# Recurrent gate and recurrent output in seven block products each, token-major, with the weight sums on GpSimd, behind the attention branch

## The chip, the cores and the metric

The kernel runs on one core of one Trainium2 chip. The metric is the time of one execution on the device in microseconds, as the median of three runs. One further execution was recorded by the hardware profiler; all rows below come from it.

## The reference, cut to what matters

One decoder layer: 256 tokens and 16 meta tokens ahead of them, width 1024, float32 throughout. A combined input projection feeds latent attention, a gated linear recurrence and two gates; their gated sum goes through an output projection, and a routed expert network follows.

```python
def reference(x, meta_tokens, ...):
    h = concatenate([meta, x], axis=1)                      # 272 tokens
    xn = rms_norm(h, norm_mix_g)
    proj = xn @ w_in                                        # columns: cq, ckv, kr, rx, rg, gates
    attn = mla_branch(proj[cq], proj[ckv], proj[kr], ...)   # ends in  o @ w_ao
    rec = rglru_branch(proj[rx], proj[rg], ...)             # ends in  y @ w_ro
    g = sigmoid(proj[..., OFF_GATE:] + b_gate)
    merged = g[..., :D_MODEL] * attn + g[..., D_MODEL:] * rec
    h = h + merged @ w_out
    h = h + moe_ffn(rms_norm(h, norm_ffn_g), ...)           # top 4 of 32 experts
    return rms_norm(h, norm_final_g)[:, N_META:]
```

Here "recurrent gate" is `sigmoid(xn @ w_in[:, gate columns D to 2D] + b_gate[D:])`, "recurrent output" is `y @ w_ro`, "attention gate" and "attention output" are their counterparts.

## The kernel before, in words

Everything is written out by hand: each engine has one instruction list, and engines wait for one another on counters (`wait_ge`, `then_inc`). The mixer's weights stream through a ring of 16 slots of 1 MB each (`ring`, filled by SyncE in the order of `LOADS`; load n goes out when `weights_used` has reached n - 15). `weights_used` is counted up by TensorE at the first matmul behind the last use of a slot. `M0` is the number of entries of `LOADS`. Behind the mixer the ring and the freed work area hold the experts' weights: 12 pieces (`RING`) of 2.1 MB for two experts at a time. The first twelve are fetched with `fetch` and `fetch_half` as slots and areas come free; the fetches of expert 2 begin when expert 0's pieces are used.

Activations are kept feature-major in the mixer (`xnT`, `gel`, `mT`: features on partitions, tokens along the row). TensorE goes through `jobs` with `project` (L607): a job is 128 output features, eight k-steps, 256 or 272 tokens wide, in PSUM bank n modulo 3. Attention runs in six steps (`attention_step`) hosted by jobs; the linear recurrence (`conv`, `recur_arg`, `recur`) runs on VectorE and ScalarE beside them. ScalarE reads the jobs in order (`read`), so a step's exponentials (`attention_exp`, L1328), which wait for VectorE's row maxima (`rowmax_ready`, L1715), stand ahead of the next job's read (L1288). VectorE walks the same list of jobs.

Then, in TensorE's order: the eight jobs of the recurrent gate (`gr`), the eight recurrent outputs (`recurrent_output`, L829), and two rounds of four attention gate jobs (`ga`) and four attention outputs (L853). ScalarE turns each gate into a tanh; VectorE multiplies it with its branch (`merge_rec`, L1739, and `merge_attn`, L1745 and L1747) and leaves the sum in `mT`.

The output projection is already done in seven products of 128x512 blocks (`product`, L889) in place of eight. `w_out` lies in four blocks of 512x512; VectorE forms five sums of them (L1776 to L1780, 128x2048 each, into `SPARE` or in place) and five sums of the blocks of `mT` (L1785 to L1789), and adds the products into `X` with weights of a half (`add_half`, L1830). Transposes of the new h (`turn_h`, L864), the router and the ranking follow, then the expert loop (L952 to L996).

GpSimd has no work of its own in the kernel.

Of the kernel before, what the change touches and what calls it, by code (L numbers as in the profile page):

```python
# [24 lines left out]
P = 128  # L25
# [111 lines left out]


OUT_BLOCKS = ((1, 1), (1, 0), (0, 0), (0, 1))
# [4 lines left out]
MIX_LANDINGS = [len(range(s, M0, SLOTS)) - (s == 0) for s in range(SLOTS)]  # L144


def load_width(kind, w):
    return {"in": KT * w, "ro": KT * w, "uq": QT * w, "ukv": KVT * w, "ao": 4 * w, "out": 4 * w, "gates": 4 * P}[kind]


def pack_mixer(g):

    packed = np.zeros((M0, P, SLOT), np.float32)
    for n, (kind, a, w) in enumerate(LOADS):
        if kind == "gates":
            both = np.stack([g["w_rg_a"][0, a:a + w], g["w_rg_x"][0, a:a + w]], axis=0)
            flat = both.transpose(2, 0, 1, 3)
        else:
            m = g[{"in": "w_in", "ro": "w_ro", "uq": "w_uq", "ukv": "w_ukv", "ao": "w_ao", "out": "w_out"}[kind]][0]
            if kind == "uq":  # L160
                heads = m.reshape(Q_LORA, 2, HEADS // 2, QD)
                m = np.concatenate([heads[..., :NOPE].reshape(Q_LORA, 2, -1), heads[..., NOPE:].reshape(Q_LORA, 2, -1)], axis=2)
                m = m.reshape(Q_LORA, HEADS * QD)
            m = m.reshape(-1, P, m.shape[1]).transpose(1, 0, 2)
            if kind == "out":
                r, c = OUT_BLOCKS[a]
# [7 lines left out]
def layer(nc, x_in, xT_in, vec_in, ca_in, cb_in, w_mix,  # L174
          norm_ffn_g, w_router, b_router, w_exp, b_up, b_down, norm_final_g, out):
    with ExitStack() as ctx:
# [84 lines left out]
        ta = view(4 * SEQ, LATE + 4736).rearrange("p (k t) -> p k t", k=4)  # L261
# [17 lines left out]
        def out_block(n):  # L279
            s = (M0 - 4 + n) % SLOTS  # L280
            return ring[:, s, :].rearrange("p (k n) -> p k n", k=4)

        w22, w21, w11, w12 = (out_block(n) for n in range(4))
        w12_22 = view(SLOT, SPARE + UNIT).rearrange("p (k n) -> p k n", k=4)
        w21_11 = view(SLOT, SPARE + UNIT + SLOT).rearrange("p (k n) -> p k n", k=4)
# [5 lines left out]
        m21_22 = ca[:, CA["mask"][0]:CA["mask"][0] + 512].rearrange("p (k t) -> p k t", k=4)  # L291
        y2 = hg
# [42 lines left out]
        def col(n):  # L335
# [71 lines left out]
            sem(n) for n in ("wsum_ready", "msum_ready", "product_done"))  # L407
        h_var, h_std, xn2_ready = (
# [32 lines left out]
        jobs += [("gr", i) for i in range(8)] + [("ga", i) for i in range(8)]  # L441
# [5 lines left out]
        hosts = [("rx", 5), ("rx", 7), ("gr", 0), ("gr", 2), ("gr", 4), ("gr", 6)]  # L447
# [4 lines left out]
        def _(spe):  # L452
# [4 lines left out]
            for n, (kind, a, w) in enumerate(LOADS):  # L457
                s = n % SLOTS
                if n == 0:
                    spe.wait_ge(head_in[1], 16)  # L460
                    continue
# [103 lines left out]
        def _(pe):  # L565
# [11 lines left out]
            def wait_load(n):  # L577
                s = slot_of(n)
                pe.wait_ge(slot_loaded[s], 16 * (n // SLOTS + (s > 0)))
# [240 lines left out]
            def recurrent_output(p):  # L820
                n = load_at[("ro", 256 * p)]
                wait_load(n)
                wv = wslot(n, KT)
                if p == 0:
                    pe.wait_ge(recurrence_done, 4)
                for i in range(2):
                    b = branch_begin()
                    for k in range(KT):
                        ins = nc.tensor.matmul(ps[:, b, 0:SEQ], wv[:, k, P * i:P * i + P], gel[:, k, :],  # L829
                                               start=(k == 0), stop=(k == KT - 1))  # L830
                        if k == 0:
                            settle(ins)
                    ins.then_inc(branch_done, 1)
                owed[0] += 1

            for p in range(4):
                for i in (2 * p, 2 * p + 1):
                    project(("gr", i), OFF_GATE + D + P * i, P, N_META, T, last=(i % 2 == 1))
                    if ("gr", i) in step_after:
                        attention_step(step_after[("gr", i)])  # L840
            for p in range(4):
                recurrent_output(p)
            for g in range(2):
                for i in range(4 * g, 4 * g + 4):
                    project(("ga", i), OFF_GATE + P * i, P, N_META, T, last=(i % 2 == 1))
# [3 lines left out]
                pe.wait_ge(attn_ready, NU)  # L849
# [8 lines left out]
                owed[0] += 1  # L858

# [24 lines left out]
            pe.wait_ge(proj_read, len(jobs))  # L884
            pe.wait_ge(wsum_ready, 5)

            def product(bank, m, w, lo=0, hi=4):
                for k in range(lo, hi):
                    ins = nc.tensor.matmul(ps[:, bank, :], m[:, k, :], w[:, k, :], start=(k == 0), stop=(k == 3))  # L889
                    if k == 0:  # L890
                        settle(ins)
                return ins

            pe.wait_ge(branch_read, KT + 4)
            product(4, m11, w12_22).then_inc(product_done, 1)
            pe.wait_ge(branch_read, 2 * KT)
            product(5, m22, w21_11).then_inc(product_done, 1)
            pe.wait_ge(msum_ready, 1)
            product(6, m11_22, w11_22).then_inc(product_done, 1)
            pe.wait_ge(msum_ready, 2)  # L900
            product(0, m11_12, w22).then_inc(weights_used, 1)
            pe.wait_ge(msum_ready, 3)
            product(1, m12, w21, 0, 2)
# [330 lines left out]

        @block.scalar
        def _(act):
# [14 lines left out]
            def read(job):  # L1251
# [44 lines left out]
                elif kind == "gr":  # L1296
# [6 lines left out]
                    ins = nc.scalar.activation(mT[:, i, :], ps[:, b, 0:SEQ], ACT.Tanh, bias=hbg[:, 8 + i:9 + i], scale=0.5)  # L1303
                else:
                    if i >= 4:
                        act.wait_ge(branch_read, 4 + i + 1)
                    ins = nc.scalar.activation(ta[:, i % 4, :], ps[:, b, 0:SEQ], ACT.Tanh, bias=hbg[:, i:i + 1], scale=0.5)
# [23 lines left out]
            def moe_loads(job):  # L1331

                kind, i = job
                if kind == "gr" and i < 4:
                    c, b = i % 2, i // 2
                    act.dma_start(bup[E * i:E * i + E, :], b_up[0, :, F * b + 512 * c:F * b + 512 * c + 512]).then_inc(moe_in, 16)
                if job == ("gr", 4):
                    act.dma_start(wr, w_router[0].rearrange("(k p) e -> p k e", p=P)).then_inc(moe_in, 16)
                if job == ("gr", 5):
                    act.dma_start(brt, b_router[0:1, :].broadcast_to([P, E])).then_inc(moe_in, 16)  # L1340
                if job == ("gr", 6):
                    act.dma_start(upper, cb_in[:, slice(*CB["upper"])]).then_inc(moe_in, 16)
                if job == ("gr", 7):
                    act.dma_start(block_base, cb_in[:, slice(*CB["block_base"])]).then_inc(moe_in, 16)
                if job == ("ga", 0):
                    act.wait_ge(attn_ready, NU)
                    act.dma_start(gffn, norm_ffn_g[0:1, :].broadcast_to([P, D])).then_inc(moe_in, 16)
                if job == ("ga", 1):
                    act.dma_start(slot_id, cb_in[:, slice(*CB["slot_id"])]).then_inc(moe_in, 16)
                if job == ("ga", 2):  # L1350
# [24 lines left out]
            for job in jobs:  # L1375
# [15 lines left out]
                if (job[0] == "rx" and job[1] % 2 == 0 and job[1] > 1) or job == ("gr", 0):  # L1391
                    input_scale(3 if job[0] == "gr" else job[1] // 2 - 1)


# [146 lines left out]
        def _(dve):  # L1541
# [194 lines left out]
            def merge_rec(i):  # L1736
                dve.wait_ge(proj_read, JOB[("gr", i)] + 1)
# [4 lines left out]
            def merge_attn(i):  # L1742
                dve.wait_ge(proj_read, JOB[("ga", i)] + 1)
                dve.wait_ge(branch_done, KT + i + 1)
                link(V.scalar_tensor_tensor(out=ta[:, i % 4, :], in0=ta[:, i % 4, :], scalar=1.0,  # L1745
                                            in1=ps[:, (7, 3)[i % 2], 0:SEQ], op0=ALU.add, op1=ALU.mult))
                V.tensor_tensor(mT[:, i, :], mT[:, i, :], ta[:, i % 4, :], ALU.add).then_inc(branch_read, 1)  # L1747


            gelu_end(0)  # L1750
            for job in jobs[JOB[("ra", 0)]:JOB[("ga", 0)]]:
                kind, i = job
                if job == ("gr", 0):
# [13 lines left out]
                if job == ("gr", 1):  # L1767
                    recur(3)
            for i in range(KT):
                merge_rec(i)  # L1770

            for n in range(4):
                s = (M0 - 4 + n) % SLOTS
                dve.wait_ge(slot_loaded[s], 16 * MIX_LANDINGS[s])
            dve.wait_ge(attn_ready, NU)
            V.tensor_tensor(w12_22, w12, w22, ALU.subtract).then_inc(wsum_ready, 1)  # L1776
            V.tensor_tensor(w21_11, w21, w11, ALU.subtract).then_inc(wsum_ready, 1)
            V.tensor_tensor(w11_22, w11, w22, ALU.add).then_inc(wsum_ready, 1)
# [247 lines left out]
```

## Time and profile before

| | |
|---|---|
| median of three runs | 1159.88 us (1159.43 to 1160.18) |
| profiled execution | 1158.32 us, span 1156.5 us |
| granted clock of TensorE | 0.998 |
| TensorE, VectorE, ScalarE, GpSimd busy | 97%, 21%, 16%, 0% of the span |
| read from memory | 440.5 MB, mean 382 GB/s with the writes |
| first `gr` job on the chain | 116.9 us |
| output products begin | 225.5 us |
| first expert matmul (L977) | 261.2 us |

The span is the time from the first to the last instruction of the profiled execution; its own time has 1.8 us more around it. A matmul of float32 appears in the records as two entries. Busy times are those of the records, and a record's duration can run past the start of the next one; the pieces of the chain do not overlap and are what durations are taken from.

### The profile page before, as it was taken

What the parts mean: (1) busy time and instruction counts of PE and PEld (TensorE: products, weight loads), DVE (VectorE), ACT (ScalarE), POOL (GpSimd) and SP (SyncE); (2) the same over time, 40 slices, a digit from 0 to 9 for tenths busy, and PEclk for the clock granted to TensorE, in tenths of its full rate; (3) what the DMA queues carried; (4) which work ended last, traced back from release to release, by engine and by line L of the source; (5) the groups of instructions that cost most, each with busy time, mean ns of one, the idle gap of its engine ahead of it and who ended that gap; (6) DMA issues with size and microseconds to landing.
All of it is one profiled execution on the core that took longest, in us unless ns stands there. A gap on an engine that the chain in (4) does not pass through costs nothing.

```text
span 1156.5 us, 13260 instructions
## 1 busy us (share of the span) xinstructions
PE 1122.5 (97%) x5576; PEld 519.7 (45%) x5576; DVE 245.2 (21%) x546; ACT 187.8 (16%) x402; POOL 0.2 (0%) x4
## 2 busy tenths in 40 slices
PE   9999999999999999999999999999998989899987
PEld 7778888753433343434333333333333333333422
DVE  5657404351111111111121111111111111111112
ACT  2466600021101010101111110101010101010102
POOL 0000000000000000000000000000000000000000
PEclk9999999999999999999999999999999999999999
DMA  9944425699999999999999999999999999999996
GB/s 346 421 179 159 160 96 224 231 334 349 429 430 430 430 427 439 430 430 433 434 433 431 433 432 432 434 434 433 432 432 432 433 433 434 433 425 430 428 428 281
DMA packets 31317, 442.13 MB, mean 382 GB/s; under 512 B 4720, under 2 KB 5232, under 8 KB 8752
## 3 DMA queue, kind: packets, MB, share of 16 engines
q1 hardware_dynamic: 28224, 438.37, 90.0%
q10 hardware_dynamic: 3056, 3.23, 0.9%
q8 instruction: 28, 0.46, 0.2%
q14 instruction: 9, 0.07, 0.0%
HBM read 440.53 MB, written 1.05 MB: 382 GB/s over the span
## 4 chain that ended last, share of the span: by engine, by line
PE 72%; DMA 25%; ACT 2%; DVE 1%; issue 0%; SPq 0%; another core or an unknown queue 0%; ACTq 0%; DVEq 0%
PE ps L977 28%; DMA work<-in_w_exp_dram 20%; PE ps L996 13%; PE ps L607 9%; DMA ring<-in_w_exp_dram 4%; PE ps L964 4%; PE ps L952 4%; PE ps L829 2%; PE ps L889 2%; PE ps L923 2%; PE ps L853 1%; ACT work L1435 1%; PE ps L692 1%; PE ps L986 1%; PE ps L645 1%; PE ps L958 1%
## 5 line engine op out<-in xcount | busy, mean ns | idle before, releaser
L977 PE MATMUL ps<-ring,work 128*64 128x512 f32 x1536 | 340.9, 595 | 12.6 <-DMA ring<-in_w_exp_dram 12.5
L977 PEld LDWEIGHTS ps<-ring,work 128*64 128x64 f32 x1536 | 108.8, 137 | 229.0 <-issue 216.0
L1921 DVE TENSOR_SCALAR work<-ps 128x512 f32<-128x512 f32 x32 | 22.1, 692 | 724.9 <-PE ps L977 724.9
L607 PE MATMUL ps<-work,ring 128*128 128x256 f32 (+1 forms) x560 | 125.9, 384 | 0.0
L977 PE MATMUL ps<-work 128*64 128x512 f32 x512 | 115.9, 596 | 3.8 <-DMA work<-in_w_exp_dram 3.8
L996 PE MATMUL ps<-ring,work 128*64 128x512 f32 x512 | 113.8, 595 | 4.0 <-ACT work L1435 3.8
L996 PE MATMUL ps<-work 128*64 128x512 f32 x504 | 112.4, 596 | 4.4 <-ACT work L1435 3.8
L607 PEld LDWEIGHTS ps<-work,ring 128*128 128x128 f32 x560 | 105.6, 190 | 17.5 <-issue 1.0
L977 PEld LDWEIGHTS ps<-work 128*64 128x64 f32 x512 | 35.1, 137 | 80.4 <-issue 73.0
L996 PEld LDWEIGHTS ps<-ring,work 128*64 128x64 f32 x512 | 35.2, 137 | 72.0 <-issue 63.0
L964 PE MATMUL ps<-work 64*128 64x512 f32 x256 | 67.5, 627 | 0.0
L996 PEld LDWEIGHTS ps<-work 128*64 128x64 f32 x504 | 34.5, 137 | 71.1 <-issue 61.9
L952 PEld LDWEIGHTS ps<-work 128*128 128x128 f32 x512 | 58.5, 192 | 14.6 <-issue 14.6
L952 PE MATMUL ps<-work 128*128 128x128 f32 x512 | 61.9, 279 | 0.0
L1430 ACT ACTIVATE work<-ps 128x256 f32<-128x256 f32 x33 | 12.7, 384 | 201.9 <-PE ps L958 196.8
L1454 ACT ACTIVATE work<-work 128x512 f32<-128x512 f32 x15 | 9.4, 630 | 206.8 <-DVE work L1921 206.8
L964 PEld LDWEIGHTS ps<-work 64*128 64x128 f32 x256 | 20.8, 185 | 45.9 <-issue 45.9
L923 PE MATMUL ps<-work 32*64 32x512 f32 x256 | 34.8, 613 | 0.0
L829 PE MATMUL ps<-work,ring 128*128 128x256 f32 x128 | 27.9, 378 | 0.0
L1435 ACT ACTIVATE work<-ps 128x256 f32<-128x256 f32 x64 | 21.1, 381 | 30.7 <-PE ps L986 28.1
L1426 ACT ACTIVATE work<-ps 128x512 f32<-128x512 f32 x32 | 19.1, 598 | 42.6 <-PE ps L952 42.6
L1459 ACT ACTIVATE work<-ps 128x512 f32<-128x512 f32 x15 | 9.0, 597 | 103.7 <-PE ps L996 103.7
(273 smaller groups left out, 636.9 us busy)
## 6 DMA issues: line engine op xcount, KB each, us to landing
ring<-in_w_exp_dram SPq DMA_DIRECT2D x40, 4096.0 KB, 42.2
work<-in_w_exp_dram SPq DMA_DIRECT2D x20, 4096.0 KB, 42.1
ring<-in_w_exp_dram SPq DMA_DIRECT2D x38, 2048.0 KB, 18.3
work<-in_w_exp_dram SPq DMA_DIRECT2D x17, 2048.0 KB, 18.8
ring<-in_w_mix_dram SPq DMA_DIRECT2D x28, 1024.0 KB, 9.0
ring<-in_w_exp_dram SPq DMA_DIRECT2D x20, 1024.0 KB, 8.3
work<-in_w_exp_dram SPq DMA_DIRECT2D x13, 1024.0 KB, 10.8
ring<-in_w_mix_dram SPq DMA_DIRECT2D x8, 256.0 KB, 13.4
```

What stands on the lines that cost most here:

```text
L607: ins = nc.tensor.matmul(ps[part:part + width, b, 0:hi - lo], wv[:, k, o:o + width], rows[:, k, lo:hi], start=(k == 0), stop=(k == KT - 1))
L829: ins = nc.tensor.matmul(ps[:, b, 0:SEQ], wv[:, k, P * i:P * i + P], gel[:, k, :], start=(k == 0), stop=(k == KT - 1))
L889: ins = nc.tensor.matmul(ps[:, bank, :], m[:, k, :], w[:, k, :], start=(k == 0), stop=(k == 3))
L923: nc.tensor.matmul(ps[CAP * c:CAP * c + CAP, b, :], sel[E * q:E * q + E, par, :], bup[E * q:E * q + E, :], start=True, stop=False)
L952: ins = nc.tensor.matmul(ps[:, bank, P * j:P * j + P], xn2[:, i, P * (4 * h + j):P * (4 * h + j) + P], pick[:, i, :, :], start=(i == 0), s ...
L964: ins = nc.tensor.matmul(ps[:, 4 + 2 * i + c, :], turned[CAP * c:CAP * c + CAP, i, :], rows[CAP * c:CAP * c + CAP, :], start=False, stop=True,
L977: ins = nc.tensor.matmul(ps[CAP * c:CAP * c + CAP, b, :], xeT[:, k, CAP * (u % 2):CAP * (u % 2) + CAP], wu[:, k % SPAN, 512 * q:512 * q + ...
L996: ins = nc.tensor.matmul(ps[CAP * c:CAP * c + CAP, bank, :], turned[:, j, CAP * g:CAP * g + CAP], wv[:, k, 512 * c:512 * c + 512], start=( ...
L1426: nc.scalar.activation(xeT[:, 4 * h:4 * h + 4, :], ps[:, bank, :].rearrange("p (j t) -> p j t", j=4), ACT.Copy).then_inc(xeT_ready, 1)
L1430: return nc.scalar.activation(turned, ps[:, bank, 0:SEQ].rearrange("p (i t) -> p i t", i=TT), ACT.Copy)
L1435: nc.scalar.activation(turned[:, 2 * h:2 * h + 2, :], ps[:, banks[h], o[h]:o[h] + 256].rearrange("p (j t) -> p j t", j=2), ACT.Copy) .then ...
L1921: V.tensor_scalar(hg, ps[:, 0, :], LIMIT, None, ALU.min).then_inc(glu_ready, 1)
```

## The change

The attention gate takes the place of the recurrent gate in the list of jobs (its eight jobs host the attention steps), both attention output rounds follow, and then the recurrent side comes in a new form, token-major: tokens on partitions, 512 features along the row.

- `w_in`'s recurrent gate columns (`gr`) and `w_ro` (`ro`) are loaded as four blocks of 512x512 each. Two entries `sum` in `LOADS` for each of them reserve a ring slot without a load, so `LOADS` grows from 36 entries to 40.
- Each of the two matrix products becomes seven `token_product`s of four k-steps, 128 tokens by 512 features. Three weight sums (`three`) and a fourth (`fourth`, after the second product) are formed by GpSimd, as are the five sums of `w_out` that VectorE formed before: 13 GpSimd operations of 128x2048.
- VectorE forms the sums of the activation blocks (`row_sums`), reads each product from PSUM and combines them (`gate_sums`, `rec_sums`), with the bias as a row that is broadcast by a new DMA on ScalarE's queue; ScalarE takes the tanh of four quarters; `gated` multiplies gate and branch.
- TensorE turns the four gated quarters back to feature-major (`turn_rec`, four transposes each) and VectorE adds them to `mT` (`add_rec`). The last quarter is turned between the second and the third output product.
- SyncE's fetches of the first two experts wait for other events; the fetch of `gffn` moves behind the second output product.

```diff
-    loads += [("in", OFF_GATE + D + 256 * p, 256) for p in range(4)]
-    loads += [("ro", 256 * p, 256) for p in range(4)]
-    for h in range(2):
-        loads += [("in", OFF_GATE + 512 * h, 256), ("in", OFF_GATE + 512 * h + 256, 256), ("ao", 512 * h, 512)]
+    loads += [("in", OFF_GATE + 256 * p, 256) for p in range(4)]
+    loads += [("ao", 512 * h, 512) for h in range(2)]
+    for g, kind in enumerate(("gr", "ro")):
+        loads += [(kind, 0, 512), ("sum", 2 * g, 0), (kind, 1, 512), (kind, 2, 512), ("sum", 2 * g + 1, 0), (kind, 3, 512)]
...
             for c in range(6):
-                if c == 5:
-                    spe.wait_ge(proj_done, len(jobs))
-                    fetch(1, 0)
                 spe.wait_ge(weights_used, M0 - SLOTS + SPAN * (c + 1))
                 fetch(0, c)
-                if c == 2:
-                    spe.wait_ge(branch_done, KT)
-                    fetch_half(1, 5, 1)
+            fetch_half(1, 5, 1)
+            spe.wait_ge(recT_done, 4)
+            fetch(1, 0)
+            fetch_half(1, 1, 0)
             spe.wait_ge(product_done, 1)
-            fetch_half(1, 1, 0)
-            spe.wait_ge(product_done, 2)
             fetch_half(1, 1, 1)
...
+            def token_product(q, m, w, frees=1):
+                if q >= 4:
+                    pe.wait_ge(token_read, q - 3)
+                product(TOKEN_BANKS[q % 4], m, w).then_inc(token_done, 1)
+                owed[0] += frees
...
+            token_product(0, x11, weight_block("gr", 0))
+            token_product(1, x12, weight_block("gr", 3), frees=0)
+            pe.wait_ge(asum_ready, 1)
+            pe.wait_ge(wsum_ready, 3)
+            token_product(2, asum[:, 1], weight_block("sum", 1), frees=0)
+            token_product(3, x21, weight_block("sum", 0))
+            token_product(4, asum[:, 0], weight_block("gr", 1))
+            token_product(5, asum[:, 2], weight_block("gr", 2))
+            pe.wait_ge(wsum_ready, 7)
+            token_product(6, x22, weight_block("gr", 3), frees=2)
...
+            token_product(7, g11, weight_block("ro", 0))
+            token_product(8, g12, weight_block("ro", 3), frees=0)
+            pe.wait_ge(asum_ready, 2)
+            token_product(9, asum[:, 1], weight_block("sum", 3), frees=0)
+            token_product(10, g21, weight_block("sum", 2))
+            pe.wait_ge(branch_read, KT)
+            turn_rec(0)
+            token_product(11, asum[:, 0], weight_block("ro", 1))
+            token_product(12, asum[:, 2], weight_block("ro", 2))
+            turn_rec(1)
+            pe.wait_ge(wsum_ready, 13)
+            token_product(13, g22, weight_block("ro", 3), frees=2)
+            turn_rec(2)
...
+        @block.gpsimd
...
+            def three(kind, g):
+                loaded(kind)
+                pool.wait_ge(weights_used, LOAD_AT[("sum", 2 * g + 1)] - SLOTS + 1)
...
+                combine(third, b22, b12, ALU.subtract)
+                combine(b12, b12, b11, ALU.subtract)
+                pool.wait_ge(wsum_ready, done[0])
+                combine(second, b22, b12, ALU.subtract)
...
+            def fourth(kind, g):
+                pool.wait_ge(token_done, 7 * g + 2)
+                b21 = weight_block(kind, 3)
+                combine(b21, weight_block("sum", 2 * g + 1), b21, ALU.subtract)
...
+            three("gr", 0)
+            three("ro", 1)
+            fourth("gr", 0)
+            loaded("out")
+            pool.wait_ge(attn_ready, NU)
+            pool.wait_ge(branch_done, KT)
+            pool.wait_ge(recurrence_done, 4)
+            combine(w12_22, w12, w22, ALU.subtract)
+            combine(w21_11, w21, w11, ALU.subtract)
+            combine(w11_22, w11, w22, ALU.add)
+            combine(w21, w21, w22, ALU.add)
+            combine(w12, w11, w12, ALU.add)
+            fourth("ro", 1)
...
+            for j in range(4):
+                act.wait_ge(gate_summed, j + 1)
+                nc.scalar.activation(quad(j), quad(j), ACT.Tanh, scale=0.5).then_inc(gate_tanh, 1)
+            act.wait_ge(product_done, 2)
+            act.dma_start(gffn, norm_ffn_g[0:1, :].broadcast_to([P, D])).then_inc(gffn_in, 16)
...
+            def row_sums(a11, a12, a21, a22):
+
+                link(V.tensor_tensor(asum[:, 0], a21, a22, ALU.add))
+                link(V.tensor_tensor(asum[:, 1], asum[:, 0], a11, ALU.subtract))
+                link(V.tensor_tensor(asum[:, 2], a12, asum[:, 1], ALU.subtract))
+                V.tensor_tensor(a21, a11, a21, ALU.subtract).then_inc(asum_ready, 1)
...
+                link(V.tensor_tensor(t1, token(2), t0, ALU.add))
...
+                link(V.tensor_tensor(t2, t1, b_step, ALU.add))
+                link(V.tensor_tensor(t0, token(3), t1, ALU.add))
+                dve.sem_inc(token_read, 1)
+                link(V.tensor_tensor(t1, t0, b_step, ALU.add))
+                V.tensor_tensor(quad(1), token(4), t1, ALU.add).then_inc(gate_summed, 1)
...
+            row_sums(x11, x12, x21, x22)
+            dve.wait_ge(bias_in, 16)
+            link(V.tensor_tensor(b_step, b_step, b_lo, ALU.subtract))
+            gate_sums()
+            row_sums(g11, g12, g21, g22)
+            rec_sums()
+            dve.wait_ge(recT_read, 2)
             V.tensor_tensor(m11_22, m11, m22, ALU.add).then_inc(msum_ready, 1)
```

`link` makes VectorE wait for its own operation before the next one.

## Rows read from the trace of the kernel before

**Rows 1.** The page: busy time by engine, transfer rate in 40 slices.
```profile
PE 1122.5 (97%) x5576; PEld 519.7 (45%) x5576; DVE 245.2 (21%) x546; ACT 187.8 (16%) x402; POOL 0.2 (0%) x4
...
GB/s 346 421 179 159 160 96 224 231 334 349 429 430 430 430 427 439 430 430 433 434 433 431 433 432 432 434 434 433 432 432 432 433 433 434 433 425 430 428 428 281
```

**Rows 2.** Windows: stretch, length, busy by engine, granted clock, DMA share, GB/s.
```profile
225.00:240.00 15.00, 15.00 (x38) 6.82 (x37) 8.88 (x18) 0.00 (x0) 0.00 (x0) 1.00 0.83 311
...
285.00:300.00 15.00, 15.00 (x74) 5.01 (x72) 0.00 (x0) 0.60 (x1) 0.00 (x0) 1.00 1.03 430
...
909.00:938.00 29.00, 26.76 (x144) 11.54 (x142) 3.78 (x8) 3.08 (x6) 0.00 (x0) 1.00 1.01 434
```

**Rows 3.** The chain that ended last: start us, us, what.
```profile
116.92 3.45 PE ps L607 x16
...
156.34 27.73 PE ps L829 x128
...
225.50 15.45 PE ps L889 x36
...
261.15 3.58 PE ps L977 x16
```

**Rows 4.** The same chain, pieces from 88 to 128 us.
```profile
94.02 0.18 DVE small L1715
...
96.72 1.73 PE ps L791 x6
...
114.98 1.94 PE ps L791 x8
...
123.20 0.81 PE ps L776 x6
```

**Rows 5.** Timeline of TensorE in the output products: start us, us, what.
```profile
240.79 0.60 PE L864 MATMUL ps<-ca,work 128*128 128x128 f32 x4
241.23 1.88 PE L889 MATMUL ps<-ring,work 128*128 128x512 f32 x4
```

**Rows 6.** Timeline of VectorE, one weight sum and two sums of `mT`.
```profile
184.51 2.29 DVE L1776 TENSOR_TENSOR work<-ring 128x2048 f32<-128x2048 f32 x1
...
226.53 0.69 DVE L1785 TENSOR_TENSOR work<-work 128x512 f32<-128x512 f32 x1
227.14 0.69 DVE L1786 TENSOR_TENSOR work<-work 128x512 f32<-128x512 f32 x1
```

**Rows 7.** Timeline of SyncE's queue, and issue to landing of L465 from 95 to 125 us.
```profile
98.94 0.80 SPq L465 DMA_DIRECT2D ring<-in_w_mix_dram  x2
...
DMA to landing us min/median/max: 4.7/4.7/7.2
...
138.91 0.33 SPq L465 DMA_DIRECT2D ring<-in_w_mix_dram  x1
...
156.80 28.06 SPq L473 DMA_DIRECT2D ring<-in_w_exp_dram  x3
```

**Rows 8.** Timeline of VectorE from 103 to 116 us.
```profile
103.73 1.58 DVE L1619 SCALAR_TENSOR_TENSOR work<-work,vec 128x272 f32<-128x272 f32 x3
...
109.92 1.08 DVE L1706 SCALAR_TENSOR_TENSOR work<-ps,ca 128x288 f32<-128x288 f32 x2
...
112.15 0.17 DVE L1715 TENSOR_SCALAR small<-small 128x4 f32<-128x4 f32 x1
...
115.73 0.35 DVE L1726 TENSOR_SCALAR work<-work,small 128x256 f32<-128x256 f32 x1
```

**Rows 9.** Timeline of ScalarE: exponentials, then the next read.
```profile
112.36 0.42 ACT L1328 ACTIVATE work<-work,small 128x144 f32<-128x144 f32 x1 [1.88 <-DVE small L1715]
...
114.18 0.36 ACT L1288 ACTIVATE work<-ps 128x256 f32<-128x256 f32 x1
```

**Rows 10.** An issue on ScalarE's queue (KB, us to landing); VectorE's first use of `gffn`.
```profile
ca<-in_ca_dram ACTq DMA_DIRECT2D x1, 505.0 KB, 8.9
...
248.97 1.29 DVE L1824 SCALAR_TENSOR_TENSOR work<-work,small 128x1024 f32<-128x1024 f32 x1
```

More of the change, by code:

```diff
@@ L276, in layer, with weight_block @@
         counts = view(E, 0)
[L279 to L285, printed above, removed]
+        def weight_block(kind, a):
+            return ring[:, LOAD_AT[(kind, a)] % SLOTS, :].rearrange("p (k n) -> p k n", k=4)
+        w22, w21, w11, w12 = (weight_block("out", n) for n in range(4))
+        w12_22 = view(SLOT, SPARE + UNIT + SLOT).rearrange("p (k n) -> p k n", k=4)
+        w21_11 = view(SLOT, SPARE + 2 * UNIT).rearrange("p (k n) -> p k n", k=4)
         w11_22 = view(SLOT, SPARE + 3 * UNIT).rearrange("p (k n) -> p k n", k=4)
@@ L440, in layer @@
                 jobs += [(kind, i) for kind in kinds for i in (2 * p, 2 * p + 1)]
-        jobs += [("gr", i) for i in range(8)] + [("ga", i) for i in range(8)]
+        jobs += [("ga", i) for i in range(8)]
         JOB = {job: n for n, job in enumerate(jobs)}
@@ L818, in branch_begin, with product @@
                 return (7, 3)[d % 2]
[L820 to L842, printed above, removed]
+            def product(bank, m, w, lo=0, hi=4):
+                for k in range(lo, hi):
+                    ins = nc.tensor.matmul(ps[:, bank, :], m[:, k, :], w[:, k, :], start=(k == 0), stop=(k == 3))
+                    if k == 0:
+                        settle(ins)
+                return ins
+            for i in range(KT):
+                project(("ga", i), OFF_GATE + P * i, P, N_META, T, last=(i % 2 == 1))
+                if ("ga", i) in step_after:
+                    attention_step(step_after[("ga", i)])
             for g in range(2):
-                for i in range(4 * g, 4 * g + 4):
-                    project(("ga", i), OFF_GATE + P * i, P, N_META, T, last=(i % 2 == 1))
                 n = load_at[("ao", 512 * g)]
@@ L881, in fold @@
                 nc.tensor.matmul(ps[:, (1, 3)[i], 0:E], logT, pick_e[:, 0:E], start=True, stop=True).then_inc(logits_done, 1)
[L884 to L894, printed above, removed]
+            pe.wait_ge(token_read, 12)
+            pe.wait_ge(recT_read, 1)
             product(4, m11, w12_22).then_inc(product_done, 1)
-            pe.wait_ge(branch_read, 2 * KT)
+            pe.wait_ge(recT_read, 2)
             product(5, m22, w21_11).then_inc(product_done, 1)
+            turn_rec(3)
             pe.wait_ge(msum_ready, 1)
@@ L1232, in _, with combine, loaded @@
                         scatter(1, y, gpickT).then_inc(more_done, 1)
+        @block.gpsimd
+        def _(pool):
+            done = [0]
+            def combine(out, a, b, op):
+                done[0] += 1
+                nc.gpsimd.tensor_tensor(out, a, b, op).then_inc(wsum_ready, 1)
+            def loaded(kind):
+                for a in range(4):
+                    n = LOAD_AT[(kind, a)]
+                    pool.wait_ge(slot_loaded[n % SLOTS], 16 * landings(n))
+            def three(kind, g):
+                loaded(kind)
+                pool.wait_ge(weights_used, LOAD_AT[("sum", 2 * g + 1)] - SLOTS + 1)
+                b11, b12, b22 = (weight_block(kind, a) for a in range(3))
+                third, second = weight_block("sum", 2 * g), weight_block("sum", 2 * g + 1)
+                combine(third, b22, b12, ALU.subtract)
[19 more added lines that the diff above has]
+            fourth("ro", 1)
         @block.scalar
@@ L1750, in _ @@
             gelu_end(0)
-            for job in jobs[JOB[("ra", 0)]:JOB[("ga", 0)]]:
+            for job in jobs[JOB[("ra", 0)]:]:
                 kind, i = job
-                if job == ("gr", 0):
+                if job == ("ga", 0):
                     gelu_end(3)
```

179 lines of the change are left out of this document (128 added, 51 removed).

## The prediction

> **What bounds the kernel now.** I read the page first, for the slices. TensorE is busy 97% of the span and the transfer rate climbs to about 430 GB/s from the ninth slice and stays there [rows 1]. Two stretches follow from it. Up to about 260 us (mixer, router) the transfer engines have room, 311 GB/s at 225 to 240 us, while TensorE is busy in all 15 us; from 285 us they are full, and late in the run TensorE is busy only 26.8 of 29 us beside a DMA share of 1.01 [rows 2]. So the expert stage is bound by transfers: its first matmul is at 261.2 us [rows 3], 30 of the 32 experts' weights (6 pieces of 2.1 MB each, 377.5 MB together) can only be fetched from about then, since the two experts ahead fill the buffers, and 377.5 MB at 432 GB/s are 874 us, which with 261 comes to 1135 us, the tail behind it. What moves the start of the expert stage by x us moves the end by x us, both ways. The chain of waits then says what sets that start: from 98 us on it is TensorE without a gap in the projections and products [rows 3], but just ahead it goes through VectorE and ScalarE: the maxima of the attention rows end at 94.2 us, ScalarE's exponentials and copies follow, and TensorE resumes at 96.7 [rows 4].
>
> **What is removed and added on TensorE.** A projection job of eight k-steps takes 3.45 us and the eight recurrent outputs 27.73 us [rows 3]. Eight gate jobs and the outputs: 27.6 + 27.7 = 55.3 us go. A projection's eight matmuls show as 16 records, two each, so the first 36 records of the output products in 15.45 us are 18 matmuls: 0.86 us each, 3.44 us a product of four [rows 3]. Fourteen products are 48.2 us. Four `turn_rec` of four transposes each: the next product starts 0.44 us behind such a group [rows 5], so 1.8 us. 55.3 - 48.2 - 1.8 = 5.3 us saved. The attention branch keeps its work and only moves; product 0 would begin at 225.5 - 55.3 = 170.2 us, t0 from here on.
>
> **VectorE's new work at its bare price.** A 128x512 operation starts 0.60 us after the one before [rows 6]. 15 of them come with the gate and 20 with the recurrent output, 21 us over 49 us; taken off are five sums of 2.3 us each [rows 6] and 16 short merges. Followed step by step against 3.44 us a product, each bank is read before it is needed again; `row_sums` on `gel` comes after token 6 (t0+24.1), so it begins at t0+24.8, ends at 27.3, and product 9 wants it at t0+31.0: 3.7 us of cover. The additions behind the last product end by +9.7 us, and the halves of h catch up about 1 us before TensorE wants the first for its transpose. Cost nothing, if VectorE runs freely.
>
> **GpSimd.** It has four instructions in the whole trace [rows 1], so no row prices its sums. From below: VectorE's 2.29 us for the same 128x2048 operation [rows 6]. From above I take double, 4.6 us, an estimate for an engine that would take its two inputs one after the other. I use the double; a sum as quick as VectorE's own, on an engine that the kernel leaves idle, seems the less likely end. In a free run the seven sums from the gate's fourth to the output's fourth lie between t0+6.9 (two products done) and t0+45.6 (product 13): covered up to 5.5 us each, so nothing is paid at either end. The Trainium skill, "GPSIMD Engine Reference", § Performance versus the Vector engine, gives 4497 ns for GpSimd and 2293 ns for VectorE at this size; the row agrees with the second, no row shows the first, and by it the sums below would be some 3% smaller.
>
> **The two engines together.** No row shows GpSimd and VectorE working at once. Bounds: they don't touch each other (0), or an operation of one with two SBUF inputs waits until the other's instruction ends. I take the second, worked out at 4.6 us an instruction, because the new GpSimd work lies exactly over VectorE's densest stretch. Two places:
>
> Place A, the gate's first three sums. The load in slot position 29 is issued at 98.9 us and lands 4.7 us later [rows 7], and `weights_used` has reached 14 by then, so `three("gr", 0)` runs from 103.6. VectorE is without a gap from 103.7 to 112.3, and up to 109.9 nearly all its work has two SBUF inputs: convolution steps, scans, products; then come L1706 (one input in PSUM) and L1713 [rows 8]. ScalarE waits in order for the row maxima (released by VectorE at 112.36) and reads the next projection only at 114.18 [rows 9]; TensorE's second `ra` job needs that read at about 115.4 and the chain has it at work from 114.98 [rows 4]. Slack 0.5 us. If each of the three instructions blocks VectorE for its full length: 3 x 4.6 - 0.5 = 13.3 us. If VectorE runs on and GpSimd gets its turn only when L1706 comes, half of the first instruction and what VectorE waits for anyway is covered; the step's probabilities, done at 116.1 us [rows 8] and wanted by the transposes at 123.2 [rows 4], have 7 us of room, and the next step's 5: 4.4 us are left by my count. No row decides the order of turns: I take 9 us.
>
> Place B, `row_sums` on `gel`. Fourth sum of the gate t0+6.9 to 11.5, then VectorE's `t2` add, sum, `t1` add, and so on in alternation: the output sums end at 16.7, 21.9, 26.5. `row_sums` from 24.8: its four linked operations each stand behind one GpSimd instruction, 27.1, 32.3, 37.5, 42.7. Product 9 waits from 31.0 to 42.7: 11.7 us. If GpSimd goes through without yielding, `t2` itself is late and product 7 waits 11 us; same price. Behind VectorE nothing else is queued that TensorE wants sooner. The early three sums of `ro` run at 144 to 158, where VectorE has next to nothing.
>
> Sum: -5.3 + 9 + 11.7 = +15.4 us on the profiled execution's 1158.3 us (span 1156.5 and 1.8 around it) = 1173.7; the median of the runs is 1.6 above that: **1175 us**.
>
> The Trainium skill, "SBUF — State Buffer", § Who interferes with whom, speaks against this change: a VectorE instruction with two SBUF inputs and a GpSimd instruction that reads SBUF exclude each other, the later one waiting for the whole of the earlier. No run here shows it; by that rule the time would be the 1175 us above, and by the profile's silence 1154.6.
>
> **Queues.** The sums take four ring positions, so SyncE's first expert fetch waits for product 3 (t0+14, 184.6 us) and no longer for 156.8, the time of its first one now [rows 7]. All six pieces of expert 0 are out by 220 us; the first half-piece of expert 1 and those after it go at 220 to 251 us, 10.5 MB of 1 MB to 2 MB each, 25 us at 430 GB/s. The last lands at about 255, when expert 0 begins (255.9). Cost 0, about 2 us of cover; each MB late would be 2.4 us. `gffn` moves to ScalarE behind product 5 (7.3 us after the output products begin); a 505 KB transfer on that queue took 8.9 us [rows 10], so it is there at +16.2, and L1824 wants it at +23.5 (248.97 less 225.5) [rows 10]. Cost 0, 7 us of cover. Behind its wait on ScalarE stands nothing due before +18.
>
> **The rivals.** (1) The engines don't disturb each other: -5.3, **1154.6 us**. For it: GpSimd is absent from the trace, so nothing contradicts it. It decides as soon as both stalls together stay under 5.3 us. (2) They take turns but the sums are short (2.29 us) or share in part: A costs 3 x 2.3 - 0.5 = 6.4 at most, B nothing (the last output sum ends at t0+22, before `row_sums`): +1.1, **1161 us**, with 1157 to 1166 around it. (3) GpSimd over 5.5 us a sum, without disturbing VectorE: product 13 waits 7 x (D - 5.5); at 6.2 us the gain is used up and the time is 1159.9. Against it: that is 2.7 times VectorE's row. (4) The saving is real but the late fetches take it: 2.2 MB of backlog, again 1159.9; against it the idle transfer time at 225 to 240 us [rows 2].
>
> **How the numbers follow.** Turns at full price: 0.52, with its own range 1166 to 1180 (A at 4.4 or 13.3). Rival 2: 0.13. Rival 1: 0.30. Rivals 3 and 4: 0.05. 0.2% is 2.3 us, about what a measurement of this kernel can tell. Faster (below 1157.6): rival 1 and a little of 2, 0.31. Same: the middle of rival 2 with 3 and 4, 0.13. Slower: 0.56. The range has to hold both rival 1 and the full price: 1154 to 1180.
>
> **What would show it.** The products' start to the first L977 matmul (35.7 us now) should stay; the stretch from the last `ga` job to the output products should be 5.3 us shorter than its counterpart, plus B. If the engines take turns, VectorE has gaps of about one GpSimd instruction ahead of two-input operations at 104 to 118 us and in `row_sums`, released by nothing that the profile names, and TensorE idles at about 115 and ahead of product 9. If GpSimd's instructions start apart by far less than 4.6 us, or VectorE shows none of these gaps, the forecast is wrong, and the time is near 1155. A long idle of TensorE might also lower its granted clock, which is 1.00 in all stretches named here [rows 2]; I give that nothing.

## The result, and the profile after

The changed kernel takes 1181.3 us (median of four runs, 1179.3 to 1182.3) against 1159.9 us before: ratio 1.0183, 95% interval 1.0165 to 1.0200, or 21.4 us slower. The forecast was 1175 us with a range to 1180; the direction was right, the size was not, and the time lies 1.3 us outside the range. The profiled execution took 1182.2 us, 23.9 us over that of before.

The page after, sections 1 and 2 (answers to [rows 1]): GpSimd now has 61 us of work, and TensorE shows two holes, in slices 5 and 8, each with a lowered granted clock in the same slice.

```profile
PE 1126.2 (95%) x5448; PEld 498.4 (42%) x5448; DVE 278.5 (24%) x560; ACT 186.8 (16%) x398; POOL 61.2 (5%) x17
...
PE   9999699699999999999999999999999999999987
...
PEclk9999799799999999999999999999999999999999
```

Waits of the changed kernel from 100 to 260 us (who waited for whom: us in total, times, longest). TensorE waits for long at two places only.

```profile
ACT work L1427 <- DVE small L1818: 14.5, 1, 14.5
...
PE ps L822 <- ACT work L1392: 12.0, 1, 12.0
...
PE ps L853 <- DVE work L1850: 10.2, 1, 10.2
```

The first is place A of the prediction: TensorE's second `ra` job waits for ScalarE's read, which stands behind the exponentials, which wait 14.5 us for VectorE's row maxima (1.88 us in [rows 9]). The second is place B: product 9 waits for `row_sums` on `gel` (L1850 is its fourth operation). TensorE's timeline at both:

```profile
116.06 0.62 PE L822 MATMUL ps<-work,ring 128*128 128x272 f32 x2
128.69 3.09 PE L822 MATMUL ps<-work,ring 128*128 128x272 f32 x6 [12.01 <-ACT work L1392]
131.57 4.61 PE L638 MATMUL ps<-work,ring 128*128 128x256 f32 x16
...
185.80 31.06 PE L853 MATMUL ps<-ring,work 128*128 128x512 f32 x72
227.07 9.84 PE L853 MATMUL ps<-ring,work 128*128 128x512 f32 x16 [10.21 <-DVE work L1850]
...
237.18 7.03 PE L853 MATMUL ps<-ring,work 128*128 128x512 f32 x16
```

Behind both holes the same work is slower: 16 records of products take 9.84 us at 227 and 7.03 us at 237, so 2.8 us more; at 128.7 the six records of `ra` and `ri` (the recurrence's own small gate matrices, L822) take 3.09 us (1.73 us at 97.97 us in the same trace) and the projection job 4.4 from its start to that of the next work at 136.01 (3.45 in [rows 3]), 2.3 us together. The windows of the changed kernel (columns as in [rows 2]) show the granted clock at 0.54 to 0.60 there, near the lower of the two levels, 1.2 GHz, and back at 1.00 from 234 us. That this is the cause was tested; see the last experiment.

```profile
129.00:134.00 5.00, 5.00 (x13) 3.89 (x13) 2.66 (x8) 3.72 (x9) 0.00 (x0) 0.54 0.11 16
218.00:227.00 9.00, 0.00 (x0) 0.00 (x0) 8.97 (x3) 0.00 (x0) 8.47 (x2) 0.55 0.07 31
227.00:234.00 7.00, 6.93 (x10) 3.02 (x11) 2.49 (x5) 0.00 (x0) 0.00 (x0) 0.60 0.00 0
234.00:249.00 15.00, 15.00 (x45) 7.25 (x44) 6.25 (x10) 0.00 (x0) 0.00 (x0) 1.00 0.53 194
```

GpSimd's timeline: ten of its thirteen sums, in the two places.

```profile
105.19 14.01 POOL L1301 TENSOR_TENSOR ring<-ring 128x2048 f32<-128x2048 f32 x3 [104.74 <-DMA ring<-in_w_mix_dram]
...
192.91 4.52 POOL L1301 TENSOR_TENSOR ring<-ring 128x2048 f32<-128x2048 f32 x1 [17.79 <-PE ps L853]
197.39 14.36 POOL L1301 TENSOR_TENSOR work<-ring 128x2048 f32<-128x2048 f32 x3
211.71 14.76 POOL L1301 TENSOR_TENSOR ring<-ring 128x2048 f32<-128x2048 f32 x3
```

And VectorE's timeline beside them, first place A, then place B. At 105 us the three convolution steps that took 1.58 us in [rows 8] take 9.87, and the product behind them 5.02; at 119.8, when GpSimd is done, the next two-input operation takes 0.72 again.

```profile
104.97 9.87 DVE L1722 SCALAR_TENSOR_TENSOR work<-work,vec 128x272 f32<-128x272 f32 x3
114.76 5.02 DVE L1795 TENSOR_TENSOR work<-work 128x544 f32<-128x544 f32 x1
119.82 0.72 DVE L1796 TENSOR_TENSOR_SCAN work<-work 128x272 f32<-128x272 f32 x1
...
199.81 0.69 DVE L1866 TENSOR_TENSOR work<-ps,work 128x512 f32<-128x512 f32 x1 [1.83 <-PE ps L853]
200.65 2.25 DVE L1868 TENSOR_TENSOR work<-work 128x512 f32<-128x512 f32 x1 [0.15 <-DVE work L1866]
...
210.87 1.43 DVE L1847 TENSOR_TENSOR work<-work 128x512 f32<-128x512 f32 x1 [0.15 <-DVE work L1874]
212.33 4.88 DVE L1848 TENSOR_TENSOR work<-work 128x512 f32<-128x512 f32 x1
217.25 4.87 DVE L1849 TENSOR_TENSOR work<-work 128x512 f32<-128x512 f32 x1
222.15 4.87 DVE L1850 TENSOR_TENSOR work<-work 128x512 f32<-128x512 f32 x1
```

Three things are to be seen. An operation `work<-work` (two inputs in SBUF) beside GpSimd lasts until about the end of the GpSimd instruction that it meets, up to 4.88 us for 0.69 us of work. An operation of the same shape with one input in PSUM (`work<-ps,work`) keeps its 0.69 us while GpSimd is busy. And the waiting stands in the *duration* of the operation, not in the idle time ahead of it: VectorE looks busy (14.9 of 15 us from 105 to 120), and no releaser is named. I had looked for gaps; there are none.

The first expert matmul (L1036) starts at 284.8 us on the chain, 23.6 us later than in [rows 3]: 12.0 and 10.2 of idle, 2.3 and 2.8 of slow clock, less 5.3 saved, make 22.0 (the 5.3 is the prediction's figure; the kernel without GpSimd, below, gives 5.5). Some 1.3 us more had arisen by 98 us, in work that both kernels share; in the eight profiles below TensorE's resumption there ([rows 4]: 96.7) lies between 97.2 and 98.1 us, in the kernel before with small additions too (97.6 and 98.1), so I take it for the scatter of single executions. 0.3 us stay unexplained.

### The profile page after: what moved, and what is told of

Read it like the earlier page. It is cut to its first block, busy times and chain, and to the rows that moved or that the text cites. A ratio compares the mean times of both kernels' runs of the same rounds, so it can differ in the third digit from the quotient of the medians.

```text
span 1180.4 us, 13044 instructions
## 1 busy us (share of the span) xinstructions
PE 1126.2 (95%) x5448; PEld 498.4 (42%) x5448; DVE 278.5 (24%) x560; ACT 186.8 (16%) x398; POOL 61.2 (5%) x17
## 4 chain that ended last, share of the span: by engine, by line
PE 80%; DMA 12%; DVE 4%; ACT 2%; issue 1%; another core or an unknown queue 0%; SPq 0%; ACTq 0%; DVEq 0%
PE ps L1036 33%; PE ps L1055 16%; DMA work<-in_w_exp_dram 11%; PE ps L638 6%; PE ps L853 6%; PE ps L1023 5%; PE ps L1011 5%; PE ps L982 2%; PE ps L869 1%; ACT work L1538 1%; PE ps L1045 1%; PE ps L1017 1%; DVE work L1722 1%; PE ps L723 1%; DMA ring<-in_w_mix_dram 1%
## 5 line engine op out<-in xcount | busy, mean ns | idle before, releaser
L1036 PE MATMUL ps<-ring,work 128*64 128x512 f32 x1536 | 344.3, 599 | 11.9 <-DMA ring<-in_w_exp_dram 11.9
L1036 PEld LDWEIGHTS ps<-ring,work 128*64 128x64 f32 x1536 | 109.8, 138 | 230.6 <-issue 219.2
L1036 PE MATMUL ps<-work 128*64 128x512 f32 x512 | 115.8, 595 | 1.9 <-DMA work<-in_w_exp_dram 1.9
L638 PE MATMUL ps<-work,ring 128*128 128x256 f32 (+1 forms) x432 | 98.9, 388 | 0.0
L638 PEld LDWEIGHTS ps<-work,ring 128*128 128x128 f32 x432 | 82.2, 192 | 14.6 <-issue 1.0
L853 PE MATMUL ps<-ring,work 128*128 128x512 f32 x136 | 62.5, 615 | 10.2 <-DVE work L1850 10.2
L1036 PEld LDWEIGHTS ps<-work 128*64 128x64 f32 x512 | 35.3, 137 | 77.8 <-issue 73.6
L1301 POOL TENSOR_TENSOR ring<-ring 128x2048 f32<-128x2048 f32 x10 | 46.7, 4688 | 165.0 <-DMA ring<-in_w_mix_dram 147.1
L853 PEld LDWEIGHTS ps<-ring,work 128*128 128x128 f32 x136 | 26.5, 198 | 42.4 <-issue 31.3
```

What stands on the lines that cost most here:

```text
L638: ins = nc.tensor.matmul(ps[part:part + width, b, 0:hi - lo], wv[:, k, o:o + width], rows[:, k, lo:hi], start=(k == 0), stop=(k == KT - 1))
L1036: ins = nc.tensor.matmul(ps[CAP * c:CAP * c + CAP, b, :], xeT[:, k, CAP * (u % 2):CAP * (u % 2) + CAP], wu[:, k % SPAN, 512 * q:512 * q + ...
L1301: nc.gpsimd.tensor_tensor(out, a, b, op).then_inc(wsum_ready, 1)
```

## The experiments

Eight kernels, on three chips, each beside the kernel before on the same chip. That took 1159.24 us beside the first four, 1159.64 beside the next three (quarters, GpSimd reading, GpSimd writing) and 1159.96 beside the last.

**Place A alone undone.** GpSimd's first three sums wait until VectorE has finished its last attention step.

```diff
+            pool.wait_ge(probs_ready, NU)
             three("gr", 0)
```

> The changed kernel with one wait more: GpSimd begins the gate's first three sums only when VectorE has finished its last attention step. Theory (the engines take turns, whole instruction by whole instruction, for operations with two SBUF inputs, and TensorE's granted clock falls while it idles): the 12.0 us idle of TensorE at 117 to 129 us and the 2.5 us that the slow clock cost behind it go, the 10.2 us ahead of product 9 and its 2.8 us stay; 1181.3 - 14.5 = 1167 us. Rival (the delay comes from the new order of branches and the new loads, GpSimd only happens to be active then): the stall stays, 1179 to 1182 us. Rival (GpSimd in this place costs only in part): between 1170 and 1178 us.

Measured: 1166.5 us, ratio 1.0066 (1.0051 to 1.0082). The stall at 117 us is gone, the one ahead of product 9 is unchanged at 10.23 us. All six early sums now run from 140.7 to 167.9 us. The reordering as such costs nothing here.

**Place B alone undone.** The two fourth sums and the five of `w_out` go to VectorE, into its waits between the products; `late_sums` counts them in order.

```diff
                 V.tensor_tensor(quad(0), token(1), t0, ALU.add).then_inc(gate_summed, 1)
+                late(weight_block("gr", 3), weight_block("sum", 1), weight_block("gr", 3), ALU.subtract)
...
                 link(V.tensor_tensor(t2, t1, b_step, ALU.add))
+                late(w12_22, w12, w22, ALU.subtract)
...
                 link(V.tensor_tensor(t1, t0, b_step, ALU.add))
+                late(w21_11, w21, w11, ALU.subtract)
...
+                late(w11_22, w11, w22, ALU.add)
                 V.tensor_tensor(quad(2), token(5), t2, ALU.add).then_inc(gate_summed, 1)
+                late(w21, w21, w22, ALU.add)
...
             row_sums(g11, g12, g21, g22)
+            late(w12, w11, w12, ALU.add)
...
                 gated(0)
+                late(weight_block("ro", 3), weight_block("sum", 3), weight_block("ro", 3), ALU.subtract)
```

> The changed kernel with the two fourth sums and the five sums of w_out on VectorE, put into its waits between the products; GpSimd keeps the six early sums. Theory of turns: row_sums on gel is free again and product 9 starts on time; 10.2 us idle and 2.8 us of slow clock go, place A stays: 1181.3 - 13.0 = 1168 us. Rival (VectorE has too much work behind the reordering, GpSimd or not): with seven sums of 2.3 us more on VectorE the products wait longer, 1181 to 1190 us.

Measured: 1167.6 us, ratio 1.0074 (1.0059 to 1.0089). Product 9 starts without a wait, the idle at place A is 11.99 us as in the changed kernel. VectorE has room for 16 us of sums more between the products: the rival of too much work falls.

**Both undone.**

> Both edits of the two runs beside it: early sums on GpSimd while VectorE rests, the late seven on VectorE. Theory of turns: both stalls and both stretches of slow clock go and only the 5.3 us saved on TensorE are left: 1181.3 - 27.5 = 1153.8, against 1159.9 - 5.3 = 1154.6 us by the forecast's own sum; so 1154 to 1155.5 us. Rival (later fetches of the experts take the saving): 1158 to 1161 us. Rival (the two stalls hide a third wait): above 1161 us.

Measured: 1153.4 us, ratio 0.9948 (0.9934 to 0.9961). The two costs add up. Counted from the kernel before on the same chip, the changed kernel is 21.4 us slower, the one without place A 7.3, the one without place B 8.3, and the one without both is 5.9 us faster: 14.1 and 13.1 us, 27.2 together, against 27.3 measured. So no third cost of that size is hidden, and the saving arrives.

**No sum on GpSimd.** The early six go to VectorE too, between its last attention step and the merges.

```diff
+            three("gr", 0)
+            three("ro", 1)
             for i in range(KT):
                 merge_attn(i)
...
-        @block.gpsimd
```

> No sum on GpSimd: the six early sums too are VectorE's, behind its last attention step, where it rests for some 18 us. Theory of turns: the same as with the early sums on a GpSimd that disturbs nobody, 1154 to 1155.5 us. Rival (VectorE is the bound once it has all the sums, 30 us more in 60): 1160 us or more, with waits of TensorE for wsum_ready.

Measured: 1152.9 us, ratio 0.9945 (0.9932 to 0.9959), 6.3 us faster than before and level with the kernel that has both places undone. GpSimd's help was never needed. Rows of the chain of this kernel, to compare with [rows 3]:

```profile
171.24 37.77 PE ps L854 x88
...
256.71 3.58 PE ps L1038 x16
```

From TensorE's resumption at 97.8 us in this trace to the first expert matmul are 158.9 us; before they were 164.4 [rows 3, 4]. 5.5 us, where the sum of the prediction has 5.3.

**The sums in quarters.** The changed kernel, each sum as four instructions of 128x512, the counts that TensorE waits for times four.

```diff
-                done[0] += 1
-                nc.gpsimd.tensor_tensor(out, a, b, op).then_inc(wsum_ready, 1)
+                for k in range(4):
+                    done[0] += 1
+                    nc.gpsimd.tensor_tensor(out[:, k, :], a[:, k, :], b[:, k, :], op).then_inc(wsum_ready, 1)
```

> The changed kernel with every GpSimd sum cut into four instructions of 128x512; same elements, same places. Theory of turns by instruction: a VectorE operation waits for one short GpSimd instruction (4.7/4 = 1.2 us), so the four of row_sums end at about t0+24.8+4x1.8=32 instead of 43 and product 9 is late by 1 us in place of 10; at place A VectorE has ten two-input operations in a row, each behind a 1.2 us instruction, so 10 to 12 us are lost as before. 1181.3 - 9 - 2.8 = 1169.5 us. Rival (shared bandwidth, in proportion to what is moved): both stalls unchanged, 1181 us.

Measured: 1165.5 us, ratio 1.0051 (1.0034 to 1.0068), 4 us below what I expected. At place B the four operations take 0.73 and three times 1.64 us, and product 9 doesn't wait at all (1 us expected). At place A TensorE still idles 8.78 us (10 to 12 expected). Same elements moved, 16 us less lost: what counts is the length of the instruction that VectorE meets, not the traffic. VectorE's timeline in this kernel:

```profile
104.29 3.35 DVE L1723 SCALAR_TENSOR_TENSOR work<-work,vec 128x272 f32<-128x272 f32 x3
107.56 1.79 DVE L1796 TENSOR_TENSOR work<-work 128x544 f32<-128x544 f32 x1
...
114.24 1.36 DVE L1720 TENSOR_SCALAR work<-work,vec 128x272 f32<-128x272 f32 x1
...
207.47 0.73 DVE L1848 TENSOR_TENSOR work<-work 128x512 f32<-128x512 f32 x1 [0.15 <-DVE work L1875]
208.24 1.64 DVE L1849 TENSOR_TENSOR work<-work 128x512 f32<-128x512 f32 x1
...
211.58 1.64 DVE L1851 TENSOR_TENSOR work<-work 128x512 f32<-128x512 f32 x1
```

In a stretch where VectorE has no pause, as at place A, the short turns add up to some three quarters of the long ones; over four operations they don't. The TENSOR_SCALAR at 114.24 has one input tensor in SBUF, with scalars per partition, and takes 1.36 us where it takes 0.42 alone (103.84 us in the same trace): two inputs are not the only form that waits.

**GpSimd reading and writing, in the kernel before.** Six subtractions on GpSimd, which read two inputs and write a result that nobody uses into a borrowed area, begun when the load in position 29 has landed. ScalarE waits for them before it first writes into that area itself; that instruction starts only at 202.9 us, released by TensorE, 82 us behind GpSimd's last (120.6), so the wait costs nothing.

```diff
+        @block.gpsimd
+        def _(pool):
+            scratch = ta.rearrange("p k t -> p (k t)")
+            pool.wait_ge(x_in_s, 16 * TT)
+            pool.wait_ge(slot_loaded[29 % SLOTS], 16 * 2)
+            for n in range(6):
+                if n:
+                    pool.wait_ge(pool_done, n)
+                nc.gpsimd.tensor_tensor(scratch, X[:, 0, :], X[:, 1, :], ALU.subtract).then_inc(pool_done, 1)
...
+                    if i == 0:
+                        act.wait_ge(pool_done, 6)
```

> The kernel before, and on GpSimd six subtractions of 128x1024 from SBUF, whose result nobody uses, begun when the load in position 29 has landed (about 103.6 us). Same GpSimd busy time as the three sums at place A, nothing else of the change. Theory of turns: VectorE's operations with two SBUF inputs wait behind them, TensorE idles 11 to 13 us at 115 us and runs on a slow clock behind it for 2.5 us: 1159.9 + 14 = 1172 to 1175 us. Rival (place A's stall belongs to the change's order or loads): 1160 us.

Measured: 1173.5 us, ratio 1.0116 (1.0099 to 1.0133). The stall of place A stands in the old kernel, without new order, new loads or products: TensorE idles 11.61 us, and the slow stretch follows with the same 3.09 us.

VectorE's timeline of this kernel, and TensorE's:

```profile
104.64 5.53 DVE L1633 SCALAR_TENSOR_TENSOR work<-work,vec 128x272 f32<-128x272 f32 x3
110.10 2.87 DVE L1706 TENSOR_TENSOR work<-work 128x544 f32<-128x544 f32 x1
```

```profile
127.96 3.09 PE L792 MATMUL ps<-work,ring 128*128 128x272 f32 x6 [11.61 <-ACT work L1301]
```

**Only GpSimd's writing.** The same as the kernel just shown, with twelve memsets of the same area (ScalarE waits for twelve).

```diff
-            for n in range(6):
+            for n in range(12):
...
-                nc.gpsimd.tensor_tensor(scratch, X[:, 0, :], X[:, 1, :], ALU.subtract).then_inc(pool_done, 1)
+                nc.gpsimd.memset(scratch, 0.0).then_inc(pool_done, 1)
```

> As the run beside it, but GpSimd only writes: twelve memsets of 128x1024 at the same place. Theory (what is shared is the way by which GpSimd reads SBUF and VectorE reads its second input): VectorE's operations keep their times, 1160 us. Rival (any GpSimd instruction on SBUF keeps VectorE out): gaps of a memset's length in front of VectorE's operations and a stall of TensorE in proportion to GpSimd's busy time.

Measured: 1159.4 us in one run, beside 1159.6 (no interval, since it is a single run; the rows carry the reading). GpSimd is at work for 12.1 us over the same operations of VectorE. Its timeline:

```profile
105.12 12.09 POOL L1244 MEMSET work<- 128x1024 f32 x12 [104.67 <-DMA ring<-in_w_mix_dram]
```

And VectorE's, where the two-input operations keep their times:

```profile
105.11 1.58 DVE L1633 SCALAR_TENSOR_TENSOR work<-work,vec 128x272 f32<-128x272 f32 x3
106.61 0.72 DVE L1706 TENSOR_TENSOR work<-work 128x544 f32<-128x544 f32 x1
...
109.35 0.92 DVE L1630 TENSOR_SCALAR work<-work,vec 128x272 f32<-128x272 f32 x1
...
116.41 0.83 DVE L1739 TENSOR_SCALAR work<-work,small 128x16 f32<-128x16 f32 x1
116.55 0.76 DVE L1740 TENSOR_SCALAR work<-work,small 128x128 f32<-128x128 f32 x1
```

Only three operations with one input tensor, all TENSOR_SCALAR, are longer: 0.92 instead of 0.42 us, and at 116.4 us, still beside GpSimd, 0.83 and 0.76 instead of 0.23 and 0.28. The two-input operations don't change. The two kernels differ in GpSimd's reading, so it is the reading that excludes VectorE's second SBUF input. Why TENSOR_SCALAR waits also beside mere writing was not tested.

**The holes filled.** The changed kernel with idle matmuls (`keep_clock`, ones by ones, result unused) where TensorE waited.

```diff
                         ins.then_inc(proj_done, 1)
+                        if (name, i) == ("ra", 6):
+                            keep_clock(3, 50)
...
+            keep_clock(6, 44)
             pe.wait_ge(asum_ready, 2)
```

> The changed kernel with matmuls of ones by ones (128x128, result unused) put where TensorE stood idle: 50 behind the first ra job of the last pair, 44 ahead of product 9. They last about 11 and 10 us, so they fit into the idle of 12.0 and 10.2 us and delay nothing. Theory (TensorE's granted clock falls while it idles, and the matmuls behind the idle pay 2.5 and 2.8 us for it): both stretches run at full clock, the stalls themselves stay; 1181.3 - 5.3 = 1176 us. Rival (the matmuls behind the stalls are slow for another reason, for instance they compete with GpSimd or wait for operands): they stay slow, 1181 us. Rival (filling lengthens the stall): above 1182 us.

Measured: 1176.9 us, ratio 1.0143 (1.0126 to 1.0160). TensorE waits 0.86 and 0.43 us behind the fillers, VectorE's operations at place B still take 4.89 us, and the granted clock is 1.00 in all four windows over the two places. TensorE's timeline at place A and place B:

```profile
116.42 11.32 PE L650 MATMUL ps<-ca 128*128 128x128 f32 x100
128.61 1.73 PE L822 MATMUL ps<-work,ring 128*128 128x272 f32 x6 [0.86 <-ACT work L1395]
...
224.74 7.13 PE L855 MATMUL ps<-ring,work 128*128 128x512 f32 x16 [0.43 <-DVE work L1853]
```

1.73 instead of 3.09 us and 7.13 instead of 9.84, with GpSimd, the loads and the order unchanged: the slow stretches came from TensorE's idle.

## Why the prediction was wrong, step by step

- **Bound.** Right. In the profiled executions the first expert matmul is 23.6 us later and the time 23.9 us longer; in the kernel without GpSimd it is 4.4 us earlier (256.7 for 261.2) and the time 4.4 us shorter (1153.88 for 1158.32). By the medians that kernel gains 6.3 us (interval 4.8 to 7.9).
- **TensorE's saving, 5.3 us.** Right: 5.5 us from the resumption to the first expert matmul; the nine products before the stall take 31.1 us, 3.44 each.
- **Queues.** Right at no cost: with both stalls gone the full saving arrives, so neither the later fetches nor `gffn` holds anything up.
- **GpSimd's sums, 4.6 us.** Right in size: 4.52 us where VectorE has no two-input operation beside them (192.9 us), 4.7 to 4.9 where it has, the turns included. The Trainium skill's 4497 ns ("GPSIMD Engine Reference", § Performance versus the Vector engine) agrees with the 4.52; it lies 2% below the 4.6 that I took, not 3% as the prediction has it.
- **The engines take turns.** Right, and now shown: by length of the instruction (quarters), by reading and not writing (the pair in the kernel before), by the number of SBUF inputs (the rows at 200 us). The rule in the Trainium skill, "SBUF — State Buffer", § Who interferes with whom, agrees with these runs in all three points: 4.88 us against 0.69 for the same operation. But the sign that the prediction names for it was wrong: it expected gaps ahead of VectorE's operations and would have taken their absence for a time near 1155 us. There are no gaps; the waiting is in the durations.
- **Place B, 11.7 us.** 10.2 measured. `row_sums` began as reckoned, 24.9 us behind product 0, but GpSimd's sum then under way ended 0.7 us earlier than reckoned, so the first operation lasted 1.4 us and not 2.3; and each of the other three turns took 4.9 us, where I had added 4.6 and 0.6.
- **Place A, 9 us.** Here a step failed. I had worked out 13.3 us for full alternation and 4.4 us for a VectorE that keeps its turn, and took a value between, as no row decided. It was alternation: VectorE met all three instructions within four operations and TensorE lost 12.0 us. The mechanism was right, the term was 3 us too small; a midpoint between two mechanisms is the price of neither. It was luck that A's 3.0 us too little and B's 1.5 us too much partly cancel: by the two stalls alone the sum is 1176.8 us, inside the range.
- **The clock, 0.** This is the step that put the time outside the range. The prediction names the fall of the granted clock in its last lines and gives it nothing. It cost 2.3 us behind place A and 2.8 behind place B, 5.1 us in all. Filling the holes shows it: 1176.9 us, 4.5 us less (the same 4.5 when each is counted from the kernel before on its own chip, 21.4 and 16.9 us). The rows of before have no price for it, since TensorE waits there for 2.0 us at the longest; but a forecast that has TensorE idle for 9 and 12 us had to carry an upper bound for the work behind them at 1.2 GHz, a few us each.

With 12.0 for 9, 10.2 for 11.7 and 5.1 for nothing the prediction's own sum gives -5.3 + 12.0 + 10.2 + 5.1 = +22.0 us, hence 1182 us; 1181.3 were measured.

The version to keep is the one without GpSimd: 1152.9 us, against 1159.2 for the kernel before on the same chip and 1181.3 for the changed one.

## What to carry to other kernels

Before work goes to an idle GpSimd, list what VectorE does in the same microseconds: each operation with two inputs in SBUF will wait for the end of whichever GpSimd instruction is reading (TENSOR_SCALAR with one waited too), so the price is paid in whole instructions, at the place where VectorE has least slack, not in a share of bandwidth. Look first for gaps in VectorE itself; 30 us of sums fitted into them here. If GpSimd must be used beside VectorE, cut its instructions short, or give VectorE operands in PSUM. And whenever a forecast has TensorE idle for several microseconds, price the work behind the idle at half clock too; here it was 2.3 and 2.8 us behind idles of 12.0 and 10.2.

## What the runs showed of the hardware that I had not expected

- The wait for GpSimd is recorded as duration of the VectorE operation (4.88 us for 0.69), so VectorE's busy share rises (14.9 of 15 us) and no view of waits shows it. A group whose mean is far above its shortest member is the sign.
- Between two GpSimd instructions that are queued back to back one VectorE operation gets through: at place B the three sums at 211.7 us and `row_sums`'s operations alternate, and GpSimd's take 4.9 instead of 4.5 us.
- Writing alone (memset) let two-input operations through unchanged, but a TENSOR_SCALAR with one SBUF input took 0.92 for 0.42 us; beside GpSimd's short subtractions the same operation took 1.36.
- Idle matmuls on constant data kept the granted clock at 1.00 through 12 us of waiting and gave back 4.5 us without lengthening the wait: from TensorE's last useful work to its next 12.0 us at place A and 10.3 at place B, for 12.0 and 10.2 without them.
